# Stick-breaking mixer: projection tiles moved against the heads, weights rounded behind each head's logarithm

## The chip, the cores and the metric

One core of a Trainium2 chip. The metric is the device time of one execution in microseconds (us), as the median of the runs of a kernel. Engines are written PE (TensorE), ACT (ScalarE), DVE (VectorE), POOL (GpSimd) and SP (SyncE).

## What is computed

Two transformer blocks run one after the other on 512 tokens of width 1024, in fp32. The change touches the mixer of the second block, a stick-breaking attention with 16 heads of 64:

```
qkv = xn @ w_qkv;  q, k = rms_norm over each head's 64;  z = q.k / 8, for s < t
log_1m = log_sigmoid(-z);  rev_excl = sum of log_1m over the keys between s and t
w = exp(log_sigmoid(z) + rev_excl);  o = w @ v;  x = x + o @ w_o
```

Everything else (two blocks' feed-forward parts with 2816 hidden units, the first mixer, the norms) is the same in both kernels.

## The kernel before

**Products in three parts.** Every fp32 matrix product is made of three float32r matmuls: a value is split into a rounded part hi and the rest lo, and hi*hi, lo*hi and hi*lo are added in PSUM (`unit`, L333 to L335; in the heads `three`, L576 to L578).

**Units.** All weights come as one stream of units of 128x1024 in four slots. SP loads a unit into `raw` (L272). ACT rounds it to `w_hi` (`round_weights`, the copy at L696, called by `ahead(u)` for unit u + 2), once the unit four before it has been used. POOL subtracts to get `w_lo` (L307), which takes the units in order, and increments `lo_done`. PE waits for `lo_done` before the first of the eight tiles of a unit (L325). One tile is three matmuls of 512 columns. SP's next load into a slot waits for the same `lo_done`.

**The second mixer.** `w_qkv` is 24 units, three to a pair of heads: the query (3t), the key (3t+1) and the value (3t+2) of pair t. `w_o` is the next eight. While the heads of pair t are computed, PE puts tiles of pair t+1 between their steps; the order is written out by hand on each engine. For a head h:

- PE: `stick_scores` (L580) into four PSUM banks, then 10 projection tiles, `weigh(h-1)` (L610, the previous head's weights times its values), `cumulate(h)` (L598, the sums over keys as matmuls with constant triangles), then 2 projection tiles. `turn_values` (L571, four transposes) stands in the even heads behind two tiles, `head_mean_square` near the end of a head.
- ACT: Abs (L904), Exp (L906) and Ln (L908) over the scores, 128x1280 each, in place of one another in `sb_e`; then rounding of values, weights and squares; the output of the previous head (`round_out`); and, when `cumulate` is done, Exp (L926).
- DVE: the softplus (L1293, one input in PSUM), its rounding `sp_hi` (L1300) and rest `sp_lo` (L1302), then values, squares, outputs and head norms; behind L926 the same split of the weights (L1316, L1318).

`cumulate(h)` waits for `sp_split`, which is `sp_lo` (L600). In an even head ACT rounds two weight units, behind `round_values`; in an odd head one, behind `head_square`. These units are 3t+5 and 3t+6, and 3t+7 (ACT lines 909 to 920): each is rounded one or two heads ahead of its first tile. The loop starts with the units 0 to 4 rounded and 0 to 2 projected. In the last two heads `out_part` (tiles of the output projection, units 24 on, whose tile k needs the heads 2k and 2k+1) takes the place of the projection.

Of the kernel before, what the change touches and what calls it, by code (L numbers as in the profile page):

```python
# [25 lines left out]
P = 128  # L26
# [4 lines left out]
QT = TOK // P  # L31
HD = 64
HEADS = 8
SB_HEADS = 16
# [4 lines left out]
AHEAD = 2  # L39
UK = 8  # L40
# [12 lines left out]
U_QKV = U_FFN3 + FFN_UNITS  # L53
U_SBO = U_QKV + QKV_UNITS
# [56 lines left out]
ENDS = [next(m for m in range(LAST_STEP + 1) if filled(m) >= UK * (n + 1)) for n in range(BETWEEN)]  # L111

FILL = [(10, 2), (10, 2)]

FAR = -1e30
OUTSIDE = -3.0e38
# [9 lines left out]
def build(nc, ctx, weights, consts, consts_b, ropes, rel, gain_cols, head_gains, x, out):  # L128
# [37 lines left out]
    at = [region]  # L166
# [151 lines left out]
    def _(pe):  # L318
# [278 lines left out]

        def cumulate(h):  # L598

            pe.wait_ge(S["sp_split"], h + 1)  # L600
            for j in range(QT):
                for k in range(j, QT):
                    to = col[j] + P * (k - j)
                    for part in sp:
                        last = pe.matmul(ps_flat[:, to:to + width[k]], (minus_upto_r if k == j else minus_ones_r),  # L605
                                         part[:, col[k]:col[k] + width[k]],
                                         start=False, stop=True, skip_group_check=True)
            last.then_inc(S["cum_done"], 1)
# [19 lines left out]
        def mixer_2():  # L628
            pairs = SB_HEADS // 2
            pe.wait_ge(S["x_updated"], DT * (FFN_RES[2] + 1))  # L630
            project(0, 2 * UK + 3)
            head_mean_square(0, 0)
            project(2 * UK + 3, 2 * UK + 5)
            head_mean_square(0, 1)
            project(2 * UK + 5, 3 * UK)
            for h in range(SB_HEADS):
                t, odd = divmod(h, 2)
                at = (3 * (t + 1)) * UK + 12 * odd
                before, behind = FILL[odd]
                stick_scores(h)  # L640
                if t + 1 < pairs:
                    if odd:
                        project(at, at + before)
                    else:
                        project(at, at + 2)
                        turn_values(t)
                        project(at + 2, at + before)
                else:
                    if not odd:
                        turn_values(t)  # L650
                    if h == SB_HEADS - 2:
                        pe.wait_ge(*evacuated_2(3 * pairs - 1))
                    if h == SB_HEADS - 1:
                        pe.wait_ge(S["sv_split"], pairs)
                    out_part(2 * odd, 0, pairs - 2)
                    out_part(2 * odd + 1, 0, 3)
                if h:
                    weigh(h - 1)
                if odd and t + 1 < pairs:
                    head_mean_square(t + 1, 1)  # L660
                cumulate(h)
                if t + 1 < pairs:
                    project(at + before, at + before + behind)
                    if not odd:
                        head_mean_square(t + 1, 0)
                else:
                    out_part(2 * odd + 1, 3, pairs - 2)
            for n in range(2):
                out_part(n, pairs - 2, pairs - 1)
            weigh(SB_HEADS - 1)  # L670
            for n in range(2, 4):
                out_part(n, pairs - 2, pairs - 1)
            for n in range(4):
                out_part(n, pairs - 1, pairs)
            for n in range(4, DT):
                out_part(n, 0, DT)
# [17 lines left out]
    def _(act):  # L694
# [163 lines left out]
        def mixer_2():  # L858
            pairs = SB_HEADS // 2

            def head_square(t, c):
                act.wait_ge(S["qk_made"], 2 * t + c + 1)
                nc.scalar.activation(scratch[:, 4 + c, :], scratch[:, c, :], ACT.Square)\
                  .then_inc(S["qk_sq_done"], 1)
                if t:
                    act.wait_ge(S["qk_ms"], 2 * t + c - 1)
                act.wait_ge(S["qk_sq_done"], 2 * t + c + 1)
                copy(qk_sq[c][0][:, :], scratch[:, 4 + c, :]).then_inc(S["qk_sq_hi"], 1)

            def head_rms(t, c):  # L870

                act.wait_ge(S["qk_ms"], 2 * t + c + 1)
                nc.scalar.activation(scratch[:, 4 + c, :], PS[:, 6 + c, :], ACT.Ln, bias=eps_col[:, 0:1])\
                  .then_inc(S["qk_ln"], 1)
                act.wait_ge(S["qk_ln"], 2 * t + c + 1)
                nc.scalar.activation(scratch[:, 4 + c, :], scratch[:, 4 + c, :], ACT.Exp, scale=-0.5)\
                  .then_inc(S["qk_inv"], 1)

            def round_values(t):
                act.wait_ge(S["sv_turned"], t + 1)  # L880
                copy(sb_v[0][:, t % 2, :, :], PS[:, 6, :].rearrange("p (i n) -> p i n", i=QT))\
                    .then_inc(S["sv_hi"], 1)

            def round_out(h):
                r = HD * (h % 2)
                act.wait_ge(S["sb_pv"], h + 1)
                copy(so_hi[r:r + HD, h // 2, :], PS[r:r + HD, 3, :]).then_inc(S["so_hi_done"], 1)

            ahead(U_QKV)
            root_mean_square(S_FFN3)  # L890
            ahead(U_QKV + 1)

            act.preload_act_table_set("natural_log_exp_and_others")
            head_square(0, 0)
            head_square(0, 1)
            ahead(U_QKV + 2)
            head_rms(0, 0)
            head_rms(0, 1)
            for h in range(SB_HEADS):
                t, odd = divmod(h, 2)  # L900
                act.wait_ge(S["z_done"], h + 1)
                if h:
                    act.wait_ge(S["w_split"], h)
                nc.scalar.activation(sb_e[:, :], ps_flat[:, 0:SBW], ACT.Abs).then_inc(S["abs_done"], 1)  # L904
                act.wait_ge(S["abs_done"], h + 1)
                nc.scalar.activation(sb_e[:, :], sb_e[:, :], ACT.Exp, scale=-1.0).then_inc(S["e_done"], 1)  # L906
                act.wait_ge(S["e_done"], h + 1)
                nc.scalar.activation(sb_e[:, :], sb_e[:, :], ACT.Ln, bias=one_col[:, 0:1]).then_inc(S["l_done"], 1)  # L908
                if not odd:
                    round_values(t)  # L910
                    if t + 1 < pairs:
                        ahead(U_QKV + 3 * (t + 1))
                        ahead(U_QKV + 3 * (t + 1) + 1)
                        head_square(t + 1, 0)
                    else:
                        ahead(U_SBO)
                        ahead(U_SBO + 1)
                elif t + 1 < pairs:
                    head_square(t + 1, 1)
                    ahead(U_QKV + 3 * (t + 1) + 2)  # L920
                if h:
                    round_out(h - 1)
                if odd and t + 1 < pairs:
                    head_rms(t + 1, 1)
                act.wait_ge(S["cum_done"], h + 1)
                nc.scalar.activation(sb_e[:, :], ps_flat[:, 0:SBW], ACT.Exp).then_inc(S["w_done"], 1)  # L926
                if not odd and t + 1 < pairs:
                    head_rms(t + 1, 0)
            round_out(SB_HEADS - 1)
            for k in range(DT):  # L930
                if k + 2 < DT:
                    ahead(U_SBO + k + 2)
                tail(k, k % 2, MIX_RES[1], T_MIX2, S_MIX2)
# [29 lines left out]
    def _(dve):  # L963
# [270 lines left out]
        def mixer_2():  # L1234
# [52 lines left out]
            zero_ssq(S_MIX2)  # L1287
            for h in range(SB_HEADS):
                t, odd = divmod(h, 2)
                if odd and t + 1 < pairs:  # L1290
                    make(t + 1, 1)
                dve.wait_ge(S["l_done"], h + 1)
                nc.vector.scalar_tensor_tensor(sb_e[:, :], ps_flat[:, 0:SBW], 0.0, sb_e[:, :], ALU.max, ALU.add)\  # L1293
                    .then_inc(S["sp_done"], 1)
                if odd and t + 1 < pairs:
                    split_squares(t + 1, 1)
                dve.wait_ge(S["sp_done"], h + 1)
                if h:
                    dve.wait_ge(S["cum_done"], h)
# [3 lines left out]
                    .then_inc(S["sp_split"], 1)  # L1303
                if not odd:
                    split_values(t)
                if not odd and t + 1 < pairs:
                    make(t + 1, 0)
                    split_squares(t + 1, 0)
                if h:
                    split_out(h - 1)  # L1310
                if odd and t + 1 < pairs:
                    head_norm(t + 1, 1)
                dve.wait_ge(S["w_done"], h + 1)
                if h:
# [2 lines left out]
                dve.wait_ge(S["w_hi_done"], h + 1)  # L1317
                nc.vector.tensor_tensor(sb_w[1][:, :], sb_e[:, :], sb_w[0][:, :].bitcast(F32), ALU.subtract)\  # L1318
                    .then_inc(S["w_split"], 1)
                if t + 1 < pairs:  # L1320
                    if odd:
                        make(t + 1, 2)
                    else:
                        head_norm(t + 1, 0)
            split_out(SB_HEADS - 1)
            for k in range(DT):
                update(k, (k + 4) % 8, U_SBO + k + 1, 1.0, MIX_RES[1], T_MIX2, S_MIX2, k % 2)
# [32 lines left out]
def mean_bank(stat):  # L1360


    return 7 if stat == S_FFN3 else 4


def index_steps(n):
# [90 lines left out]
```

## Time and profile before

| | us |
|---|---|
| median of 3 runs (2284.69 to 2287.91) | 2285.65 |
| the profiled execution's own time | 2284.73 |
| its span in the trace | 2282.9 |
| PE busy | 2215.4 |
| ACT, DVE, POOL busy | 778.8, 813.9, 867.7 |

The profiled execution lies 0.9 us below the median, and its span 1.8 us below its own time. The mixer's first scores start 1573 us into the span; its output projection ends at 1913. In the trace, idle time stands in square brackets with what ended it. The granted clock (PEclk) is 1.00 where TensorE has its full 2.4 GHz and 0.50 at 1.2 GHz. The ends of matmuls are modelled: one of 512 columns is shown as 0.39 us while the next starts 0.23 us after it.

### The profile page before, as it was taken

The page shows a single profiled execution, that of the slowest core. Times are in us where ns is not written, and L with a number is a line of the kernel's source. Part 1 is how long each engine was busy: PE and PEld are TensorE (multiplying, and loading weights), DVE is VectorE, ACT ScalarE, POOL GpSimd, SP SyncE. Part 2 cuts the span into 40 slices and gives each one's busy share as a digit, 9 for nine tenths or more (in the row PEclk, how much of TensorE's full clock was granted, in tenths as well). Part 3 has the DMA queues.
Part 4 walks back from the last instruction along what each step waited for, and adds up shares of the span by engine and source line. Part 5 has one row for each costly group of instructions (what it writes and reads, how often), then busy time and mean ns, then how long its engine had stood idle before and what let it go on. Part 6 is the DMA issues. An engine that isn't in the chain of part 4 may idle for free. (4 is left out here: it accounts for less than half of the span.)

```text
span 2282.9 us, 27488 instructions
## 1 busy us (share of the span) xinstructions
PE 2215.4 (97%) x9986; PEld 1800.9 (79%) x9986; DVE 813.9 (36%) x1159; ACT 778.8 (34%) x1065; POOL 867.7 (38%) x363
## 2 busy tenths in 40 slices
PE   7999999999999999999999999998989898999999
PEld 6888887676777888888878888887777777888887
DVE  5222112586322432222125222114677655222200
ACT  4223222234333442222333232224545544232221
POOL 4444444331222444444544444443121214444443
PEclk9999999999999999999999999999999999999999
DMA  4332324211111222323332322332111102322332
GB/s 156 101 101 92 110 98 138 81 65 38 51 52 56 92 92 94 103 98 101 103 100 93 101 92 92 106 106 74 37 47 37 47 28 83 101 92 92 101 116 78
DMA packets 56045, 196.53 MB, mean 86 GB/s; under 512 B 6384, under 2 KB 6768, under 8 KB 55984
## 3 DMA queue, kind: packets, MB, share of 16 engines
q1 hardware_dynamic: 54720, 192.93, 25.6%
q10 hardware_dynamic: 1264, 2.75, 0.4%
q8 instruction: 43, 0.70, 0.1%
q14 instruction: 18, 0.15, 0.0%
HBM read 193.43 MB, written 2.10 MB: 86 GB/s over the span
## 5 line engine op out<-in xcount | busy, mean ns | idle before, releaser
L307 POOL TENSOR_TENSOR w_lo<-raw,w_hi 128x1024 fp32r<-128x1024 f32 x359 | 867.5, 2428 | 1396.4 <-ACT w_hi L696 1395.0
L333 PE MATMUL ps<-xn_hi,w_hi 128*128 128x512 f32 x1912 | 765.4, 400 | 17.4 <-DVE xn_lo L997 9.2
L334 PE MATMUL ps<-xn_lo,w_hi 128*128 128x512 f32 x1912 | 748.2, 391 | 0.0
L335 PE MATMUL ps<-xn_hi,w_lo 128*128 128x512 f32 x1912 | 748.2, 391 | 0.0
L333 PEld LDWEIGHTS ps<-xn_hi,w_hi 128*128 128x128 f32 x1912 | 361.2, 189 | 126.0 <-issue 41.9
L335 PEld LDWEIGHTS ps<-xn_hi,w_lo 128*128 128x128 f32 x1912 | 360.9, 189 | 76.8
L334 PEld LDWEIGHTS ps<-xn_lo,w_hi 128*128 128x128 f32 x1912 | 361.7, 189 | 73.4 <-issue 2.6
L696 ACT ACTIVATE w_hi<-raw 128x1024 fp32r<-128x1024 f32 x359 | 364.7, 1048 | 129.9 <-PE ps L335 118.3
L965 DVE TENSOR_TENSOR scratch<-ps,rstd 128x512 f32<-128x512 f32 x207 | 142.6, 690 | 594.1 <-PE ps L335 593.6
L333 PE MATMUL ps<-h_hi,w_hi 128*128 128x512 f32 x704 | 274.0, 389 | 0.0
L334 PE MATMUL ps<-h_lo,w_hi 128*128 128x512 f32 x704 | 274.0, 389 | 0.0
L335 PE MATMUL ps<-h_hi,w_lo 128*128 128x512 f32 x704 | 274.0, 389 | 0.0
L696 ACT ACTIVATE h_hi<-scratch 128x512 f32 (+1 forms) x88 | 55.6, 632 | 476.1 <-DVE scratch L965 476.1
L1058 DVE SCALAR_TENSOR_TENSOR x_sb<-ps,x_sb 128x512 f32 (+1 forms) x48 | 33.1, 690 | 412.0 <-PE ps L335 412.0
L335 PEld LDWEIGHTS ps<-h_hi,w_lo 128*128 128x128 f32 x704 | 132.2, 188 | 27.4
L333 PEld LDWEIGHTS ps<-h_hi,w_hi 128*128 128x128 f32 x704 | 132.2, 188 | 27.3
L334 PEld LDWEIGHTS ps<-h_lo,w_hi 128*128 128x128 f32 x704 | 132.2, 188 | 27.3
L758 ACT ACTIVATE scratch<-scratch 128x512 f32<-128x512 f32 x88 | 55.6, 632 | 180.1 <-DVE scratch L965 180.1
L732 ACT ACTIVATE scratch<-x_sb 128x512 f32 (+1 forms) x40 | 25.3, 632 | 267.4 <-DVE x_sb L1058 267.4
L1012 DVE TENSOR_TENSOR h_lo<-scratch,h_hi 128x512 f32 (+1 forms) x88 | 61.0, 693 | 80.4 <-ACT h_hi L696 80.4
L605 PE MATMUL ps<-sp_hi,const_r 128*128 128x128 f32 (+3 forms) x160 | 54.8, 361 | 33.3 <-DVE sp_lo L1302 33.3
L605 PEld LDWEIGHTS ps<-sp_hi,const_r 128*128 128x128 f32 x160 | 38.0, 237 | 38.8 <-DVE sp_lo L1302 37.8
(179 smaller groups left out, 1832.1 us busy)
## 6 DMA issues: line engine op xcount, KB each, us to landing
raw<-weights SPq DMA_DIRECT2D x359, 512.0 KB, 3.4
x_sb<-x_t SPq DMA_DIRECT2D x8, 256.0 KB, 6.0
bias<-rel ACTq DMA_DIRECT2D x1, 2048.0 KB, 10.1
out_t<-x_sb SPq DMA_DIRECT2D x8, 256.0 KB, 4.7
rope<-ropes ACTq DMA_DIRECT2D x1, 512.0 KB, 3.6
const<-consts SPq DMA_DIRECT2D x1, 192.0 KB, 7.3
to_round<-consts SPq DMA_DIRECT2D x1, 192.0 KB, 7.5
ki<-ki ACTq DMA_DIRECT2D x1, 128.0 KB, 2.2
```

The source lines that it names most:

```text
L307: nc.gpsimd.tensor_tensor(w_lo[s][:, :, :], raw[s][:, :, :], w_hi[s][:, :, :].bitcast(F32), ALU.subtract).then_inc(S["lo_done"], 1)
L333: pe.matmul(to, w_hi[s][:, k, :], hi, start=opens, stop=False)
L334: pe.matmul(to, w_hi[s][:, k, :], lo, start=False, stop=False)
L335: last = pe.matmul(to, w_lo[s][:, k, :], hi, start=False, stop=ends)
L605: last = pe.matmul(ps_flat[:, to:to + width[k]], (minus_upto_r if k == j else minus_ones_r), part[:, col[k]:col[k] + width[k]], start=Fals ...
L696: return nc.scalar.activation(dst, src, ACT.Copy)
L732: nc.scalar.activation(scratch[:, 4 + b, :], X[:, k, :], ACT.Square).then_inc(S["sq_done"], 1)
L758: nc.scalar.activation(scratch[:, j, :], scratch[:, j, :], ACT.Silu).then_inc(S["silu_done"], 1)
L965: return nc.vector.tensor_tensor(dst, p, q, ALU.mult)
L1012: nc.vector.tensor_tensor(h_lo[:, F, :], scratch[:, 2 + j, :], h_hi[:, F, :].bitcast(F32), ALU.subtract).then_inc(S["h_lo_done"], 1)
L1058: nc.vector.scalar_tensor_tensor(X[:, k, :], PS[:, bank, :], factor, X[:, k, :], ALU.mult, ALU.add).then_inc(S["x_updated"], 1)
```

## The change

Head h has the same number of tiles as before, 12 to a head, but six tiles more are done ahead of the loop, so every tile stands six places earlier against the heads: an even head now has the last two tiles of unit 3t+3, all of 3t+4 and two of 3t+5, and an odd head the other six of 3t+5 and six of 3t+6. `head_mean_square` stands behind `cumulate` in the even heads. `cumulate` takes all products with `sp_hi` first, and waits for `sp_lo` only for the second half. ACT rounds unit 5 ahead of the loop; in the loop the weights that `rounded_behind(h - 1)` names are rounded right behind head h's Ln: unit 3t+6 in an odd head, 3t+4 and 3t+5 in an even one (none in head 0), and 24 in head 13, 25 to 27 in head 14. DVE moves projections, squares and norms in the same way, and `split_out(h-1)` behind the split of head h's weights. In the last heads the parts of the output projection stand in another order.

The diff's core, in the order PE, ACT (from `head_rms(0, 0)` on), DVE (from the removed `make(t + 1, 1)` on), new function:

```diff
-FILL = [(10, 2), (10, 2)]
...
 def cumulate(h):
-            pe.wait_ge(S["sp_split"], h + 1)
-            for j in range(QT):
-                for k in range(j, QT):
-                    to = col[j] + P * (k - j)
-                    for part in sp:
+            for part, ready in ((sp[0], S["sp_hi_done"]), (sp[1], S["sp_split"])):
+                pe.wait_ge(ready, h + 1)
+                for j in range(QT):
+                    for k in range(j, QT):
+                        to = col[j] + P * (k - j)
...
-            project(2 * UK + 5, 3 * UK)
+            project(2 * UK + 5, 3 * UK + 6)
             for h in range(SB_HEADS):
                 t, odd = divmod(h, 2)
-                at = (3 * (t + 1)) * UK + 12 * odd
-                before, behind = FILL[odd]
+                at = 3 * (t + 1) * UK
+                more = t + 1 < pairs
                 stick_scores(h)
-                if t + 1 < pairs:
-                    if odd:
-                        project(at, at + before)
+                if not odd:
+                    if more:
+                        project(at + 6, at + 8)
+                    turn_values(t)
+                    if more:
+                        project(at + 8, at + 16)
                     else:
-                        project(at, at + 2)
-                        turn_values(t)
-                        project(at + 2, at + before)
+                        pe.wait_ge(*evacuated_2(3 * pairs - 1))
+                        out_part(1, 0, pairs - 2)
+                        out_part(3, 0, 4)
+                elif t + 2 < pairs:
+                    project(at + 18, at + 28)
+                elif more:
+                    project(at + 18, at + 24)
+                    out_part(0, 0, 4)
                 else:
-                    if not odd:
-                        turn_values(t)
-                    if h == SB_HEADS - 2:
-                        pe.wait_ge(*evacuated_2(3 * pairs - 1))
-                    if h == SB_HEADS - 1:
-                        pe.wait_ge(S["sv_split"], pairs)
-                    out_part(2 * odd, 0, pairs - 2)
-                    out_part(2 * odd + 1, 0, 3)
+                    pe.wait_ge(S["sv_split"], pairs)
+                    out_part(2, 0, pairs - 2)
+                    out_part(0, pairs - 2, pairs - 1)
                 if h:
                     weigh(h - 1)
-                if odd and t + 1 < pairs:
+                cumulate(h)
+                if not odd and more:
+                    head_mean_square(t + 1, 0)
+                    project(at + 16, at + 18)
                     head_mean_square(t + 1, 1)
-                cumulate(h)
-                if t + 1 < pairs:
-                    project(at + before, at + before + behind)
-                    if not odd:
-                        head_mean_square(t + 1, 0)
-                else:
-                    out_part(2 * odd + 1, 3, pairs - 2)
-            for n in range(2):
+                elif not odd:
+                    out_part(3, 4, pairs - 2)
+                elif t + 2 < pairs:
+                    project(at + 28, at + 30)
+                elif more:
+                    out_part(0, 4, pairs - 2)
+            for n in range(1, 4):
                 out_part(n, pairs - 2, pairs - 1)
             weigh(SB_HEADS - 1)
-            for n in range(2, 4):
-                out_part(n, pairs - 2, pairs - 1)
...
             head_rms(0, 0)
             head_rms(0, 1)
+            ahead(U_QKV + 3)
...
                 nc.scalar.activation(sb_e[:, :], sb_e[:, :], ACT.Ln, bias=one_col[:, 0:1]).then_inc(S["l_done"], 1)
+                for n in rounded_behind(h - 1):
+                    ahead(U_QKV + n - AHEAD)
                 if not odd:
+                    if more:
+                        head_square(t + 1, 0)
                     round_values(t)
-                    if t + 1 < pairs:
-                        ahead(U_QKV + 3 * (t + 1))
-                        ahead(U_QKV + 3 * (t + 1) + 1)
-                        head_square(t + 1, 0)
-                    else:
-                        ahead(U_SBO)
-                        ahead(U_SBO + 1)
-                elif t + 1 < pairs:
-                    head_square(t + 1, 1)
-                    ahead(U_QKV + 3 * (t + 1) + 2)
+                elif more:
+                    head_rms(t + 1, 1)
                 if h:
                     round_out(h - 1)
-                if odd and t + 1 < pairs:
-                    head_rms(t + 1, 1)
+                if not odd and more:
+                    head_square(t + 1, 1)
...
-                if odd and t + 1 < pairs:
-                    make(t + 1, 1)
+                if not odd and more:
+                    make(t + 1, 0)
...
-                if odd and t + 1 < pairs:
-                    split_squares(t + 1, 1)
...
                 if not odd:
                     split_values(t)
-                if not odd and t + 1 < pairs:
-                    make(t + 1, 0)
-                    split_squares(t + 1, 0)
-                if h:
-                    split_out(h - 1)
-                if odd and t + 1 < pairs:
+                    if more:
+                        split_squares(t + 1, 0)
+                        make(t + 1, 1)
+                        split_squares(t + 1, 1)
+                elif more:
+                    head_norm(t + 1, 0)
                     head_norm(t + 1, 1)
...
-                if t + 1 < pairs:
-                    if odd:
-                        make(t + 1, 2)
-                    else:
-                        head_norm(t + 1, 0)
+                if odd and more:
+                    make(t + 1, 2)
+                if h:
+                    split_out(h - 1)
...
+def rounded_behind(h):
+
+    t, odd = divmod(h, 2)
+    first = 3 * (t + 2)
+    if h < 0 or h >= SB_HEADS - 3:
+        return range(first + 1, first + 4) if h == SB_HEADS - 3 else range(0)
+    return range(first + 1, first + 3) if odd else range(first, first + 1)
```

## Rows read from the trace of the kernel before

**Rows 1.** The page, part 1: busy us, share of the span, instructions.
```profile
PE 2215.4 (97%) x9986; PEld 1800.9 (79%) x9986; DVE 813.9 (36%) x1159; ACT 778.8 (34%) x1065; POOL 867.7 (38%) x363
```

**Rows 2.** Waits of PE, 1560 to 1900 us: total us, times, longest.
```profile
PE ps L605 <- DVE sp_lo L1302: 33.3, 15, 3.1
PE ps L576 <- DVE sb_k_lo L1263: 2.8, 1, 2.8
PE ps L333 <- POOL w_lo L307: 1.6, 1, 1.6
...
PE ps L576 <- DVE sb_w_lo L1318: 0.2, 1, 0.2
```

**Rows 3.** Timeline of an even head, ACT, DVE, POOL: start, us, engine, line.
```profile
1691.36 1.24 ACT L904 ACTIVATE sb_e<-ps 128x1280 f32<-128x1280 f32 x1 [2.60 <-PE ps L595]
...
1693.94 1.37 ACT L908 ACTIVATE sb_e<-sb_e,one_col 128x1280 f32<-128x1280 f32 x1
...
1695.34 1.49 DVE L1293 SCALAR_TENSOR_TENSOR sb_e<-ps,sb_e 128x1280 f32<-128x1280 f32 x1 [3.59 <-ACT sb_e L908]
1695.68 2.00 ACT L696 ACTIVATE w_hi<-raw 128x1024 fp32r<-128x1024 f32 x2
...
1696.81 5.29 POOL L307 TENSOR_TENSOR w_lo<-raw,w_hi 128x1024 fp32r<-128x1024 f32 x2 [13.71 <-ACT w_hi L696]
...
1696.87 3.03 DVE L1300 CAST sp_hi<-sb_e 128x1280 fp32r<-128x1280 f32 x1
1699.93 3.52 DVE L1302 TENSOR_TENSOR sp_lo<-sb_e,sp_hi 128x1280 fp32r<-128x1280 f32 x1
```

**Rows 4.** Timeline of PE in the same head.
```profile
1691.05 0.27 PE L595 MATMUL ps<-const_b 128*128 128x256 bf16 x1
...
1692.54 0.60 PE L571 MATMUL ps<-const,scratch 128*128 128x128 f32 x4
1692.89 0.47 PE L333 MATMUL ps<-xn_hi,w_hi 128*128 128x512 f32 x1
...
1694.36 0.39 PE L333 MATMUL ps<-xn_hi,w_hi 128*128 128x512 f32 x1
...
1695.04 0.39 PE L333 MATMUL ps<-xn_hi,w_hi 128*128 128x512 f32 x1
...
1703.51 0.79 PE L605 MATMUL ps<-sp_hi,const_r 128*128 128x512 f32 x1 [3.04 <-DVE sp_lo L1302]
```

**Rows 5.** The next, odd head, and all of POOL's instructions by duration.
```profile
1717.33 1.04 ACT L696 ACTIVATE w_hi<-raw 128x1024 fp32r<-128x1024 f32 x1
...
1718.22 0.82 DVE L1300 CAST sp_hi<-sb_e 128x1280 fp32r<-128x1280 f32 x1
...
1718.45 2.84 POOL L307 TENSOR_TENSOR w_lo<-raw,w_hi 128x1024 fp32r<-128x1024 f32 x1 [16.35 <-ACT w_hi L696]
...
L307 POOL TENSOR_TENSOR w_lo<-raw,w_hi x359: 2340/2400/2942, 5.5 to 2261.9; 128x1024 fp32r<-128x1024 f32 x180
```

**Rows 6.** Stretches: us; PE, PEld, DVE, ACT, POOL busy; granted clock; DMA.
```profile
1573.00:1864.00 291.00, 257.19 (x1287) 218.56 (x1288) 199.52 (x174) 145.17 (x161) 62.17 (x23) 0.93 0.13 42
...
1703.40:1706.60 3.20, 3.10 (x10) 2.91 (x11) 1.78 (x4) 1.80 (x3) 0.00 (x0) 0.50 0.40 154
...
1723.40:1726.80 3.40, 3.40 (x25) 3.12 (x23) 1.62 (x3) 1.08 (x1) 0.00 (x0) 1.00 0.20 82
1573.70:1580.30 6.60, 6.60 (x24) 5.68 (x24) 0.34 (x1) 3.46 (x3) 0.00 (x0) 0.50 0.01 2
1583.00:1592.00 9.00, 5.88 (x34) 4.98 (x33) 7.54 (x5) 1.40 (x4) 4.52 (x2) 1.00 0.34 117
```

**Rows 7.** Timeline of the last head's end, ACT and DVE.
```profile
1878.95 1.24 ACT L926 ACTIVATE sb_e<-ps 128x1280 f32<-128x1280 f32 x1 [2.34 <-PE ps L605]
...
1881.09 1.49 DVE L1318 TENSOR_TENSOR sb_w_lo<-sb_e,sb_w_hi 128x1280 fp32r<-128x1280 f32 x1
1884.80 0.59 ACT L696 ACTIVATE so_hi<-ps 64x512 fp32r<-64x512 f32 x1 [4.61 <-PE ps L578]
1885.43 0.69 DVE L1274 TENSOR_TENSOR so_lo<-ps,so_hi 64x512 fp32r<-64x512 f32 x1 [2.85 <-ACT so_hi L696]
```

More of the change, by code:

```diff
@@ L898, in mixer_2 @@
             head_rms(0, 1)
+            ahead(U_QKV + 3)
             for h in range(SB_HEADS):
                 t, odd = divmod(h, 2)
+                more = t + 1 < pairs
                 act.wait_ge(S["z_done"], h + 1)
@@ L1289, in mixer_2 @@
                 t, odd = divmod(h, 2)
-                if odd and t + 1 < pairs:
-                    make(t + 1, 1)
+                more = t + 1 < pairs
+                if not odd and more:
+                    make(t + 1, 0)
                 dve.wait_ge(S["l_done"], h + 1)
@@ L1305, in mixer_2 @@
                     split_values(t)
-                if not odd and t + 1 < pairs:
-                    make(t + 1, 0)
-                    split_squares(t + 1, 0)
-                if h:
-                    split_out(h - 1)
-                if odd and t + 1 < pairs:
+                    if more:
[4 more added lines that the diff above has]
+                    head_norm(t + 1, 0)
                     head_norm(t + 1, 1)
```

## The prediction

> **What bounds the kernel now.** I read the page first: PE is busy for 2215.4 of 2282.9 us [rows 1], so what an edit is worth is read from PE's idle time and from its clock. The waits of PE over the mixer come next: 33.3 us in 15 waits before `cumulate`, all for `sp_lo`, then 2.8 before the first scores, and 1.6 and 0.2 near the end [rows 2]. The timeline of an even head shows why the longest are 3.0 us: POOL's two subtractions and DVE's `sp_hi` and `sp_lo` run at the same time, and DVE's take 3.03 and 3.52 us [rows 3] where `sp_hi` takes 0.82 in an odd head, in which it starts before POOL [rows 5]. L1293, which reads PSUM, takes 1.49 beside nothing and is not held up [rows 3]. PE arrives 3.04 us early [rows 4]. The stretches show a second price: behind the 2.8 us wait the clock is 0.50 for 6.6 us, behind the 3.04 us wait for 3.2 us; it stays 1.00 about the first head's 3.1 us wait and behind a short one of 1.3 us [rows 6]. The mean of 0.93 over 291 us [rows 6] means 0.07 x 2 x 291 = 41 us at 1.2 GHz, which is eight falls of 5.1 us; about 38 of them are busy time, so 19 us are lost to it.
>
> **What the change takes away.** With six tiles more ahead of the loop (6 x 0.68 = 4.1 us, the pitch of a tile being 1695.04 - 1694.36 [rows 4]), the first scores wait less. But unit 5's subtraction now runs about 1570.6 to 1573.0, in the middle of the second head norm, and holds up its last three DVE steps (0.75, 0.43 and 0.69 us by the neighbouring steps' sizes, an estimate): 0.8 of the 2.8 us stay. The waits for `sp_lo` all go (33.3 us), as the next part shows: PE comes to `cumulate` later than `sp_lo` ends. The split of `cumulate` in two halves, costed at nothing, is hidden by that same lateness.
>
> **What it adds: the weights come late.** `rounded_behind(h - 1)` names the units that head h itself uses. In an odd head unit 3t+6 is rounded behind that head's Ln and its first tile is the seventh of the ten in front; in an even head from the third on unit 3t+4 is rounded there and its first tile stands behind only two tiles and four transposes. I count from the end of the scores, Z = 1691.05 + 0.27 = 1691.32 [rows 4]. Ln ends at 1693.94 + 1.37 = 1695.31 [rows 3], Z + 4.0. The rounding takes 1.04 and POOL starts 0.08 behind it (1717.33 + 1.04 against 1718.45) [rows 5]; a subtraction by itself takes 2.40, the median of 359 [rows 5]. DVE's `sp_hi` comes only behind L1293's 1.49 us, 0.4 us behind POOL's start, so POOL goes first. Ready: Z + 4.0 + 1.04 + 0.08 + 2.40 = Z + 7.5.
>
> - Even heads 2 to 12, six of them: PE is at this unit at 1692.89 [rows 4], Z + 1.6. It waits 5.9, shown as some 5.6 since the modelled end lies later.
> - Odd heads 1 to 13, seven: six tiles, Z - 0.2 + 4.1 = Z + 3.9; it waits 3.6, shown as 3.3.
> - Head 14: `out_part(1)` needs unit 25 behind the transposes alone: 6.4; and unit 27, the third of three subtractions, another 0.8 (less than its lateness, as PE's six tiles between are at the low clock).
> - Sum: 6 x 5.6 + 7 x 3.3 + 6.4 + 0.8 = 63.9 us.
>
> What stands behind these waits: on PE the rest of the head, `weigh`, `cumulate` and the next scores, and behind them ACT's Exp (L926) and Abs; nothing can make it up, since both chains start from the same scores. `sp_lo` is hidden: in an even head 8 tiles and `weigh` took from 1692.89 to 1700.47 (1703.51 - 3.04) [rows 4], 7.6 us, so PE reaches `cumulate` at Z + 15.1, and `sp_lo` ended at Z + 12.1 (1699.93 + 3.52) [rows 3]. In an odd head 4 tiles and `weigh` put it at Z + 12.3, `sp_lo` at about Z + 9.8. The late unit of an even head also makes its key squares late, but these are needed only behind `cumulate`.
>
> **The end.** Behind the last `cumulate`, Exp, `sb_w_hi`, `sb_w_lo` end at 1881.09 + 1.49 = 1882.58, 3.6 us behind 1878.95 [rows 7]. Now `split_out(14)` with 0.69 comes behind that, and PE has three tiles, 2.05, instead of five: 2.2 us of wait instead of 0.2. Behind the last `weigh` no tile is left to cover `so_hi` and `so_lo`, 0.59 + 0.69 with their hand-offs from 1884.76 to 1886.12 [rows 7]: 1.3 us. Together +3.3. The 1.6 us for POOL stays.
>
> **Moved at no cost.** Unit 5's rounding one step earlier: ACT has its two norm steps done by then. Its load and the next one of SP's queue, and POOL's turn, come earlier by it; POOL is busy 62 of 291 us here [rows 6]. The loads of later units are triggered by later subtractions, but each slot is still filled a head or more ahead. `head_square`, `head_rms`, `make` and the squares on ACT and DVE lie under PE's longer head. DVE is busy for 199.5 of 291 us [rows 6]; if the cover went, `sp_lo` would be late next.
>
> **The clock.** The trace has no waits of 3.3 and 5.6 us in front of projections. The bounds: nothing more than now (the same eight falls), or every one of 14 such waits followed by a long stretch, 14 x 6.6 / 2 = 46, 27 more than now. Eight of nine waits of 2.8 to 3.1 us were followed by a fall, so I take 14 falls; and for each the shorter length, 3.4 us, as in a longer wait a part of the slow stretch lies in the wait: 14 x 3.4 / 2 = 24, which is 4.6 more than the 19.2 of now (38.4 / 2).
>
> **Sum.** Idle: 63.9 + 0.8 - 2.8 - 33.3 + 3.3 = +31.9. Clock +4.6. Together +36.5 on the profiled execution's own 2284.7; the median lies 0.9 above it: 2285.65 + 36.5 = 2322.1 us, slower by 1.6%.
>
> **Rivals.**
>
> - **The units are there in time** (faster). If a unit's subtraction ended before PE comes to it, that is within 1.6 us of the scores in an even head and 3.9 in an odd one, only the gain would be left. It takes PE's 33.3 to about 0.9 in each even head (`cumulate`'s second half at Z + 10.8 against `sp_lo` at Z + 11.7), 7 in all, and leaves no wait that lowers the clock: -26.3 - 2.0 + 3.3 - 19.2 = -44, 2241 us. For it: POOL is idle for four fifths and was waited for once [rows 2, 6]. Against: Ln alone ends at Z + 4.0 [rows 3], and ACT goes in order, so no unit of this head can be rounded before. If the new function does something else than I read (units of the next head), this would be the case. 3%.
> - **The odd heads' waits don't lower the clock** because they lie unluckily, as the first head's 3.1 us did: seven falls fewer, 7 x 3.4 / 2 = 12 less: 2310 us. 9%.
> - **The slow stretches are the long ones**: +27 instead of +4.6: 2345 us. For it: the 6.6 us behind the first scores [rows 6]. 8%.
> - **POOL is slowed beside DVE.** A subtraction next to `sp_hi` took 2.84 instead of 2.40 [rows 5]. If all 14 late units met this: 14 x 0.44 = +6.2, 2328 us. Against: in the odd row DVE had started 0.23 us before POOL, and now POOL would be 0.4 us ahead. The Trainium skill bears on this one in a sentence of its own: "GPSIMD Engine Reference", "Specifications", says that GpSimd shares its SBUF interfaces with VectorE and contends with instructions in a two-port mode or with two SBUF inputs; read as a rule for every overlap it gives this rival's 2328 rather than 2322. By that rule, which the trace bears out with 1.49 us for L1293 in every head, the first subtraction is free of DVE for the 0.4 us. 12%.
>
> **How the numbers follow.** My own case has 67%. The likeliest case gives 2322. The range takes in the third and fourth case by half of the clock's bound, 2322 + 14 = 2336, and goes down past the second to 2309; the 3% of a gain and most of the longest clock case lie outside. About 0.2%, 4.6 us, is what a measurement of this kernel can tell from no change: slower by more than that 0.96, within it 0.01, faster 0.03.
>
> **What would show it.** Right: waits of PE's L333 on POOL's `w_lo` L307 of about 64 us in some 15 pieces, 3.3 in the odd and 5.6 in the even heads; none of L605 on `sp_lo` or a few tenths; POOL's `w_lo` starting 5.1 us behind the scores in every head; 14 stretches at 0.50. It ends with a wait of L576 on DVE of about 2.2. Wrong: waits on POOL below 10 us, which would mean that the units were rounded a head earlier; or waits as forecast with a clock of 1.00 behind them, or of 0.50 through half of the mixer.

## The result and the profile after

The changed kernel takes 2321.57 us (median of 4 runs, 2320.59 to 2324.08) against 2285.66 before: the ratio is 1.0157, with a 95% interval of 1.014 to 1.0175. It is slower by 35.9 us; the forecast was 36.5.

Page, part 1, after, behind its first line. It answers to [rows 1]: PE is busy 5.8 us longer, and the span is 39.4 us longer, so 33.6 us of it are idle time. The profiled execution was the slowest of the four.

```profile
span 2322.3 us, 27488 instructions
...
PE 2221.2 (96%) x9986; PEld 1801.0 (78%) x9986; DVE 807.6 (35%) x1159; ACT 777.8 (33%) x1065; POOL 864.8 (37%) x363
```

Waits of PE in the mixer, 1560 to 1960 us, after (total, times, longest), against [rows 2]. L331, L574 and L603 are the former L333, L576 and L605; L305 is POOL's subtraction, the former L307.

```profile
PE ps L331 <- POOL w_lo L305: 59.8, 15, 5.7
PE ps L331 <- issue: 6.3, 1, 6.3
...
PE ps L574 <- DVE so_lo L1273: 2.3, 1, 2.3
PE ps L331 <- DVE so_lo L1273: 1.4, 1, 1.4
PE ps L574 <- DVE sb_k_lo L1262: 0.8, 1, 0.8
```

The 33.3 us of waits for `sp_lo` are gone from the list: no wait of L603 is left. In their place stand 59.8 us for `w_lo`; 1.6 of them are the old wait near the end, and the 6.3 us that the view puts down to "issue" are head 14's wait for unit 25, whose `w_lo` ends in that moment. Late weights cost 59.8 - 1.6 + 6.3 = 64.5 us.

The timeline of an even head after, the one that [rows 3, 4] show of before; the first fence is ACT, DVE and POOL, the second PE.

```profile
1707.57 1.36 ACT L911 ACTIVATE sb_e<-sb_e,one_col 128x1280 f32<-128x1280 f32 x1
1708.84 1.99 ACT L697 ACTIVATE w_hi<-raw 128x1024 fp32r<-128x1024 f32 x2
1708.96 1.49 DVE L1293 SCALAR_TENSOR_TENSOR sb_e<-ps,sb_e 128x1280 f32<-128x1280 f32 x1 [1.90 <-ACT sb_e L911]
1709.96 5.26 POOL L305 TENSOR_TENSOR w_lo<-raw,w_hi 128x1024 fp32r<-128x1024 f32 x2 [17.97 <-ACT w_hi L697]
1710.49 2.50 DVE L1298 CAST sp_hi<-sb_e 128x1280 fp32r<-128x1280 f32 x1
...
1713.03 3.54 DVE L1300 TENSOR_TENSOR sp_lo<-sb_e,sp_hi 128x1280 fp32r<-128x1280 f32 x1
```

```profile
1704.69 0.27 PE L593 MATMUL ps<-const_b 128*128 128x256 bf16 x1
...
1706.18 0.60 PE L569 MATMUL ps<-const,scratch 128*128 128x128 f32 x4
1712.46 0.76 PE L331 MATMUL ps<-xn_hi,w_hi 128*128 128x512 f32 x1 [5.68 <-POOL w_lo L305]
...
1721.36 1.54 PE L603 MATMUL ps<-sp_hi,const_r 128*128 128x512 f32 x10
```

The scores end at 1704.96. Ln ends 4.0 us later, POOL starts 1.0 behind it, and the first tile of the late unit runs at 1712.46, 7.5 us behind the scores. `cumulate` starts at 1721.36 with no idle time ahead of it; `sp_lo` had ended at 1716.57, 4.8 us earlier. The odd heads show the same with 3.4 us of wait.

Stretches after (us; PE, PEld, DVE, ACT, POOL busy; granted clock; DMA), against [rows 6]: the whole of the heads, and the first scores with what follows.

```profile
1573.00:1904.00 331.00, 265.22 (x1302) 220.79 (x1301) 193.06 (x176) 142.32 (x159) 58.89 (x23) 0.89 0.12 38
1576.00:1584.00 8.00, 7.16 (x33) 5.97 (x33) 3.12 (x6) 4.39 (x4) 0.00 (x0) 0.79 0.22 66
```

A mean of 0.89 means 0.11 x 2 x 331 = 73 us at 1.2 GHz, where it was 41. Much of it lies in the waits, in which it costs nothing.

### The profile page after: what moved, and what is told of

Same layout as the page of the kernel before. It is cut to its first block and busy times, and to the rows that moved or that the text cites. A ratio compares the mean times of both kernels' runs of the same rounds, so it can differ in the third digit from the quotient of the medians.

```text
span 2322.3 us, 27488 instructions
## 1 busy us (share of the span) xinstructions
PE 2221.2 (96%) x9986; PEld 1801.0 (78%) x9986; DVE 807.6 (35%) x1159; ACT 777.8 (33%) x1065; POOL 864.8 (37%) x363
## 3 DMA queue, kind: packets, MB, share of 16 engines
q1 hardware_dynamic: 54720, 192.93, 25.1%
## 5 line engine op out<-in xcount | busy, mean ns | idle before, releaser
L305 POOL TENSOR_TENSOR w_lo<-raw,w_hi 128x1024 fp32r<-128x1024 f32 x359 | 864.6, 2420 | 1438.6 <-ACT w_hi L697 1437.1
L331 PE MATMUL ps<-xn_hi,w_hi 128*128 128x512 f32 x1912 | 773.5, 405 | 72.3 <-POOL w_lo L305 54.3
L333 PE MATMUL ps<-xn_hi,w_lo 128*128 128x512 f32 x1912 | 753.7, 394 | 0.0
L331 PEld LDWEIGHTS ps<-xn_hi,w_hi 128*128 128x128 f32 x1912 | 365.4, 191 | 186.2 <-issue 91.3
L333 PEld LDWEIGHTS ps<-xn_hi,w_lo 128*128 128x128 f32 x1912 | 364.3, 191 | 78.9
L331 PE MATMUL ps<-h_hi,w_hi 128*128 128x512 f32 x704 | 274.0, 389 | 0.0
L333 PE MATMUL ps<-h_hi,w_lo 128*128 128x512 f32 x704 | 274.0, 389 | 0.0
L331 PEld LDWEIGHTS ps<-h_hi,w_hi 128*128 128x128 f32 x704 | 132.2, 188 | 27.4
L333 PEld LDWEIGHTS ps<-h_hi,w_lo 128*128 128x128 f32 x704 | 132.2, 188 | 27.2
L964 DVE TENSOR_TENSOR scratch<-scratch 128x512 f32<-128x512 f32 x89 | 61.8, 695 | 9.2
L697 ACT ACTIVATE scratch<-ps 128x128 f32<-128x128 f32 (+3 forms) x64 | 27.8, 434 | 89.5 <-PE ps L507 89.4
```

Of the source, the lines that this page charges most:

```text
L305: nc.gpsimd.tensor_tensor(w_lo[s][:, :, :], raw[s][:, :, :], w_hi[s][:, :, :].bitcast(F32), ALU.subtract).then_inc(S["lo_done"], 1)
L331: pe.matmul(to, w_hi[s][:, k, :], hi, start=opens, stop=False)
L333: last = pe.matmul(to, w_lo[s][:, k, :], hi, start=False, stop=ends)
L697: return nc.scalar.activation(dst, src, ACT.Copy)
L964: return nc.vector.tensor_tensor(dst, p, q, ALU.mult)
```

## The experiments

For each run I split the span of its profiled execution into PE's busy time and the rest (page, part 1). As all kernels run the same 9986 matmuls, I read a difference in busy time as what the clock costs; it resolves some 2 us, since e2 and e9 differ by 1.7 with an edit that cannot touch it.

| kernel | time, us | span | PE busy | rest |
|---|---|---|---|---|
| before | 2285.66 | 2282.9 | 2215.4 | 67.5 |
| changed | 2321.57 | 2322.3 | 2221.2 | 101.1 |
| e1, next head's units behind Ln | 2260.17 | 2258.6 | 2206.6 | 52.0 |
| e2, the same units behind the second Exp | 2239.67 | 2237.9 | 2199.1 | 38.8 |
| e3, before with halves | 2261.89 | 2261.0 | 2210.6 | 50.4 |
| e4, odd heads' units early | 2293.34 | 2292.7 | 2215.5 | 77.2 |
| e5, before, rounding first | 2276.75 | 2276.3 | 2213.3 | 63.0 |
| e6, spread rounding | 2251.05 | 2249.4 | 2198.9 | 50.5 |
| e7, e2 without halves | 2241.87 | 2239.3 | 2198.5 | 40.8 |
| e8, e6 with unit 5 in the loop | 2251.30 | 2250.6 | 2201.3 | 49.3 |
| e9, e2 with the end mended | 2237.85 | 2236.1 | 2197.4 | 38.7 |
| e10, even heads' units early | 2273.73 | 2272.6 | 2209.3 | 63.3 |

**e1: the same place, the next head's units.** The changed kernel with one argument changed.

```diff
-                for n in rounded_behind(h - 1):
+                for n in rounded_behind(h):
                     ahead(U_QKV + n - AHEAD)
```

> The changed kernel, but behind head h's logarithm the units of head h+1 are rounded, not those of head h (the new function is called with h). Theory (the late units are the whole loss): no wait of PE on POOL inside the heads; an odd head now has two subtractions beside its softplus split, so the second half of its cumulate waits about 1.8 us (7 x 1.8 = 12 us); no low clock in the heads but the one behind the first scores; about 2247 us. Rival (the loss lies in the new order of the tiles or in POOL running beside DVE right behind the logarithm): waits move to sp_lo in the same size as before, 33 us, and the low stretches stay; about 2285 us or more.

2260.17 us, ratio to before 0.9887 (0.9869 to 0.9904). The waits for weights in the heads are gone, and with them 61 us against the changed kernel. So what costs is above all which unit is rounded there; the place itself is worth the 20.5 us by which e2 is faster. The time is 13 us above the expectation. Part of it stands in the waits of PE (1560 to 1960 us):

```profile
PE ps L603 <- DVE sp_lo L1300: 11.6, 7, 1.7
PE ps L574 <- DVE sb_k_lo L1262: 5.7, 5, 2.8
```

The seven waits for `sp_lo` came as expected; the second line did not. Two subtractions in an odd head push the head norms back, and the next scores wait for them; the 2.8 us are behind head 13, which has three. Most of the rest is the clock: PE is busy 7.5 us longer than in e2. It did not stay up behind every 1.7 us wait, against what I wrote, while it did behind the first scores, where I had a fall. The granted clock in the 3.3 us behind the second and the third of these waits:

```profile
1641.30:1644.60 3.30, 3.30 (x13) 3.06 (x14) 3.16 (x6) 0.93 (x1) 0.00 (x0) 0.58 0.38 139
1676.70:1680.00 3.30, 3.03 (x16) 2.38 (x16) 3.16 (x6) 1.25 (x1) 0.00 (x0) 1.00 0.38 139
```

**e2: the same units at the end of the head before.**

```diff
                 nc.scalar.activation(sb_e[:, :], sb_e[:, :], ACT.Ln, bias=one_col[:, 0:1]).then_inc(S["l_done"], 1)
-                for n in rounded_behind(h - 1):
-                    ahead(U_QKV + n - AHEAD)
...
                 if not odd and more:
                     head_rms(t + 1, 0)
+                for n in rounded_behind(h):
+                    ahead(U_QKV + n - AHEAD)
```

> The changed kernel, but the same units are rounded at the end of the head before, behind its second Exp, away from the softplus split. Theory: units in time and POOL nowhere beside sp_hi and sp_lo, so no wait in the heads at all, no low clock behind them: 2285.7 - 33.3 - 2.0 + 3.3 (the end) - 17.5 (clock) = about 2236 us. Rival (the rounding at this place delays ACT's Abs of the next head, or POOL holds up the split of the weights): a wait of some 1 to 2 us in each head turns up on another line, 2250 to 2265 us.

2239.67 us, ratio 0.980 (0.9783 to 0.9818). PE's waits in the heads are six of 0.4 us for `w_lo`, and 1.0 and 0.3 in head 14; the clock from 1573 to 1820 us is 0.99. The expected 2236 left these small waits out: a subtraction that starts 0.12 us behind the second step of the weights' split takes 3.62 us instead of 2.40, while the split keeps its 1.49 (last two rows, from the timelines). Against the changed kernel this moves nothing but the roundings, and is 82 us faster.

```profile
PE ps L331 <- POOL w_lo L305: 4.4, 8, 1.6
PE ps L574 <- DVE so_lo L1273: 2.3, 1, 2.3
PE ps L331 <- DVE so_lo L1273: 1.4, 1, 1.4
PE ps L331 <- issue: 1.0, 1, 1.0
```

```profile
1639.33 1.49 DVE L1316 TENSOR_TENSOR sb_w_lo<-sb_e,sb_w_hi 128x1280 fp32r<-128x1280 f32 x1
1639.45 3.62 POOL L305 TENSOR_TENSOR w_lo<-raw,w_hi 128x1024 fp32r<-128x1024 f32 x1 [12.54 <-ACT w_hi L697]
```

**e4 and e10: one kind of late unit at a time.** The changed kernel; in e4 the odd heads' unit is rounded in the even head before, in e10 (`if odd:` in place of `if not odd:`) the even heads' units in the odd head before.

```diff
-                for n in rounded_behind(h - 1):
-                    ahead(U_QKV + n - AHEAD)
+                if not odd:
+                    for n in (*rounded_behind(h - 1), *rounded_behind(h)):
+                        ahead(U_QKV + n - AHEAD)
```

> The changed kernel, but the unit that an odd head needs is rounded in the even head before it, behind the even head's own units; only the even heads' units come late. Theory: the seven waits of 3.4 us go with their seven low stretches (1.65 us each), the even heads' waits of 5.7 us stay: 2321.6 - 23.6 - 11.5 = about 2286 us. Rival (a 5.7 us wait brings a longer low stretch when no other is near it): 2290 to 2300 us.

> The mirror of the run in which the odd heads' units were early: here only the odd heads' unit comes late, and the even heads' units are rounded behind it in the same odd head. Theory: seven waits of 3.4 us stay, the 5.7 us ones go; three subtractions in an odd head push sp_lo and the head norms back, so that some 1.5 us of wait for sb_k_lo come before six of the next scores; with low clock behind each 3.4 us wait at 1.7 us lost or more: 2239.7 + 24 + 12 to 16 + 9 = 2285 to 2289 us. Rival (a 3.4 us wait lowers the clock only where a 5.7 us wait stands near it): about 2273 us.

e4: 2293.34 us, ratio 1.0036 (1.0024 to 1.0047). e10: 2273.73, ratio 0.9948 (0.9933 to 0.9963). Waits of PE for `w_lo`, first e4, then e10:

```profile
PE ps L331 <- POOL w_lo L305: 35.0, 7, 5.7
PE ps L331 <- issue: 6.3, 1, 6.3
```

```profile
PE ps L331 <- POOL w_lo L305: 25.1, 8, 3.4
PE ps L574 <- DVE sb_k_lo L1263: 4.9, 3, 3.1
```

The waits are the expected ones, six of 5.7 us and head 14's in e4, seven of 3.4 in e10 (25.1 less the old 1.6 is 23.5). In e4 the rest falls by 23.9 us against the changed kernel, 23.6 expected. The clock is what both missed. Busy time above that of e2 is 16.4 us in e4 and 10.2 in e10; I had put 11.5 us of gain on the odd heads in e4 and it was 5.7. In e10 I had also doubled the waits for `sb_k_lo`, 9 for a measured 4.1 above the first scores' 0.8, and had added the late waits to e2's time without taking off the small ones that they replace, some 3 us.

e4's time is that of its rival, and the rows bear it out in five of the seven late heads. Behind the ends of the late waits PE is busy at 0.50 for 3.8, 5.1, 5.8, 6.1, 2.9, 4.7 and 5.6 us, 34 in all, so 17 us are lost, 2.4 a head; the changed kernel has 3.1 to 3.3 behind the same waits. Their length is the same, so the length alone does not set the price: the slow stretch starts 3.0, 1.7, 1.0, 0.7, 0.5, 2.2 and 4.6 us ahead of the wait's end, and only what is left of it behind the end is paid. Here are the first late wait, from 1611.95 to 1617.63, from the inside and behind it, and the time behind the fourth, which ended at 1738.15. Whether the odd heads' waits decide where a stretch starts was not tried.

```profile
1615.00:1617.00 2.00, 0.00 (x0) 0.00 (x0) 1.97 (x2) 2.00 (x4) 1.87 (x1) 0.50 0.00 0
1617.70:1621.00 3.30, 3.30 (x8) 2.62 (x9) 3.27 (x2) 0.97 (x2) 3.27 (x2) 0.50 0.48 159
1738.15:1744.29 6.14, 6.14 (x15) 4.79 (x16) 6.11 (x4) 1.04 (x2) 6.14 (x2) 0.50 0.51 171
```

The rival of e10, that short waits lower the clock only beside long ones, names the measured time but falls: behind each of e10's first three 3.4 us waits the clock is 0.58 to 0.69 on the mean of some 3.3 us. In all a fall follows five of the seven; the fourth and the seventh have none. These are the first and the fourth.

```profile
1600.60:1604.00 3.40, 3.40 (x10) 2.64 (x11) 3.37 (x2) 0.48 (x1) 3.40 (x2) 0.58 0.48 159
1712.30:1715.60 3.30, 3.30 (x15) 2.67 (x15) 3.27 (x2) 0.33 (x1) 3.26 (x2) 1.00 0.51 159
```

**e3 and e5: two parts of the change alone, in the kernel before.** e3 takes over the two halves of `cumulate`, as the change has them. e5 rounds the units of before directly behind Ln:

```diff
                 if not odd:
+                    ahead(U_QKV + 3 * (t + 1))
+                    ahead(U_QKV + 3 * (t + 1) + 1)
                     round_values(t)
                     if t + 1 < pairs:
-                        ahead(U_QKV + 3 * (t + 1))
-                        ahead(U_QKV + 3 * (t + 1) + 1)
                         head_square(t + 1, 0)
...
                 elif t + 1 < pairs:
+                    ahead(U_QKV + 3 * (t + 1) + 2)
                     head_square(t + 1, 1)
-                    ahead(U_QKV + 3 * (t + 1) + 2)
```

> The kernel before with one part of the change alone: cumulate takes the products with sp_hi first and waits for sp_lo behind them. Theory: the hi half (10 matmuls, 1.4 us) fills the 1.3 us waits of the odd heads and leaves 1.6 us of the 3.0 in the even ones: -20 us of idle time; waits of 1.6 us don't lower the clock, another -16: about 2250 us. Rival (the clock falls behind 1.6 us waits as well): about 2266 us. Rival (sp_hi itself ends too late to help in the even heads): about 2275 us.

> The kernel before with another part of the change alone: the same units as before are rounded directly behind each head's logarithm, ahead of the values and the squares. Theory: POOL starts 0.5 us earlier in the even heads and about 1 us in the odd ones, and now goes ahead of sp_hi in both; sp_lo ends 0.3 us earlier in the even heads (POOL's two subtractions still stand around it) and 0.7 in the odd ones: 7 to 8 us of waits fewer, the low stretches as before, about 2278 us. Rival (the place directly behind the logarithm itself holds up the softplus split, by POOL): later by up to 1.6 us in each odd head, 2290 to 2297 us.

e3: 2261.89 us, ratio 0.9897 (0.988 to 0.9915). The time lies between the expected 2250 and the rival's 2266. The waits for `sp_lo` fall to 13.8 us in 8 pieces (expected 13), all in even heads. But the clock falls behind some of the 1.7 us waits and not behind others, so each of the two cases holds in part: the first row is behind the wait that ended at 1695.18, the second behind the one at 1730.82.

```profile
1695.20:1698.50 3.30, 3.30 (x12) 3.11 (x13) 1.85 (x4) 2.00 (x4) 0.00 (x0) 0.52 0.41 150
1730.90:1734.00 3.10, 2.96 (x16) 2.31 (x16) 1.68 (x3) 1.86 (x4) 0.00 (x0) 1.00 0.38 145
```

e5: 2276.75 us, ratio 0.9961 (0.9945 to 0.9976). The time is the expected 2278 within 2 us, but the waits for `sp_lo` are 28.6 us instead of 33.3, 4.7 less where I had put 7 to 8. Rounding right behind Ln is a small gain by itself (0.4%) as long as the units are those of a later head. Both parts are sound; neither is what made the changed kernel slow.

**e6 and e8: two attempts to better e2 that failed.** e6 rounds an odd head's first unit ahead of the second Exp and puts `split_out(14)` back in front of the last split; e8 moves unit 5 into head 0 as well.

```diff
+                if odd:
+                    for n in rounded_behind(h)[:1]:
+                        ahead(U_QKV + n - AHEAD)
                 act.wait_ge(S["cum_done"], h + 1)
```

> The kernel that rounds behind the second Exp, with two changes: in odd heads the first of the units is rounded already behind the rounding of the previous head's output, ahead of the second Exp; and split_out(14) stands ahead of the split of the last head's weights. Theory: the seven waits of 0.4 us and the 1.3 us of head 14 go, and 0.7 us at the end: 2239.7 - 4.9 = about 2235 us. Rival (POOL's subtraction now holds up the head norms or the split of the weights on DVE, so that the next scores are late): 2240 us or more.

> As the run with spread rounding and the mended end, but unit 5 is rounded in head 0 behind the values and not ahead of the loop, so that its subtraction no longer stands in the second head norm. Theory: the 0.84 us wait before the first scores goes, and the low stretch behind these scores (3.4 us, 1.7 lost) with it: 2.5 us less than that run, about 2232.5 us. Rival (the clock falls behind these scores without any wait, since their matmuls use 64 of 128 rows): only 0.8 us less.

2251.05 and 2251.30 us (ratios 0.9844, 0.9831 to 0.9857, and 0.985, 0.9837 to 0.9864). e6's rival came true. Its timeline at the end of an odd head, POOL and DVE:

```profile
1637.85 2.40 POOL L305 TENSOR_TENSOR w_lo<-raw,w_hi 128x1024 fp32r<-128x1024 f32 x1 [9.15 <-ACT w_hi L697]
1637.94 2.60 DVE L1263 CAST sb_k_hi<-scratch 128x512 fp32r<-128x512 f32 x1
...
1641.26 2.97 POOL L305 TENSOR_TENSOR w_lo<-raw,w_hi 128x1024 fp32r<-128x1024 f32 x1 [1.01 <-ACT w_hi L697]
1642.04 3.55 DVE L1321 TENSOR_TENSOR sb_w_lo<-sb_e,sb_w_hi 128x1280 fp32r<-128x1280 f32 x1
```

`sb_k_hi`, 0.43 us by itself, takes 2.60, and `sb_w_lo`, 1.49 by itself, takes 3.55: each started 0.1 to 0.8 us behind a subtraction and ended with or after it. The next scores wait 0.9 us for `sb_k_lo` and the transposes 1.1 for the values. In e8 the first scores wait for nothing, but unit 5's subtraction now holds up the squares; what it gains (rest -1.2) the clock takes back. The stretch at 0.50 that both of its cases were about was not there to be had: behind e6's first scores the clock is 1.00, for all its wait of 0.85 us.

**e7 and e9: parts of e2.** e7 takes the halves out of e2, e9 puts `split_out(14)` ahead of the last head's split.

```diff
+                if h == SB_HEADS - 1:
+                    split_out(h - 1)
                 dve.wait_ge(S["w_done"], h + 1)
...
-                if h:
+                if 0 < h < SB_HEADS - 1:
                     split_out(h - 1)
```

> The kernel that rounds behind the second Exp, with cumulate as before: hi and lo in turn, one wait for sp_lo. Theory: sp_lo ends 7.9 us behind the scores and PE comes to cumulate at 8.7 or later, so the halves bring nothing there: 2239 to 2241 us. Rival (the halves still cover something in the first or last heads): 2241 to 2245 us.

> The kernel that rounds behind the second Exp, with one change: split_out(14) stands ahead of the split of the last head's weights, as it did before the change. Theory (the 2.3 us wait before the last weigh is 3.6 us of Exp and split plus 0.7 of split_out, less three tiles): that wait is 1.6 us, 0.7 us less in all, about 2239.0 us. Rival (the last weights' split waits for split_out in turn, since both are DVE's): no change, 2239.7.

e7: 2241.87 us, ratio 0.981 (0.9796 to 0.9823). The intervals of e2 and e7 overlap, so the waits decide: those for `sp_lo` are 0.7 us in head 0 and 1.3 in head 15 and were nothing in e2, so the halves are worth 2 us there, the rival's case; I had overlooked that head 0 has no `weigh` and head 15 fewer tiles. e9: 2237.85 us, ratio 0.9797 (0.9784 to 0.9811). The wait before the last `weigh` is 1.6 us instead of 2.3, as expected; the rest of its 1.8 us against e2 is not resolved (their profiles differ by 1.7 us of busy time, which the edit cannot touch). It is the fastest version here, 48.0 us below the kernel before as run beside it (2285.88) and 83.7 below the changed one.

## Why the prediction was right

**The late units, 63.9 us: 64.5 measured.** The count from the scores (4.0 + 1.04 + 0.08 + 2.40 = Z + 7.5) met the timeline to 0.1 us. Single waits: 5.7 in the even heads (5.6 forecast), 3.4 in the odd (3.3), 6.3 in head 14 (6.4), 0.6 for unit 27 (0.8). e1 and e2 show the cause: with the next head's units in place of this head's, these waits go.

**The waits for `sp_lo`, -33.3: gone**, and hidden by the margin that I worked out: `cumulate` came 4.8 us behind `sp_lo`, where 3.0 was forecast (PE 1.3 us later, as the tiles behind its wait ran at the low clock, and `sp_lo` 0.5 us earlier).

**The first scores, 0.8 of 2.8 us left: 0.8. The end, +3.3: +3.5** (2.3 + 1.4 against 0.2). The e9 run shows the `split_out` part by itself.

**The clock, +4.6: about +5.** The rest of the span's 39.4 us divides so: the mixer starts 1.8 us later than in the profiled execution of before, PE's waits in the mixer add 71.1 - 38.4 = 32.7 (with 0.5 for the transposes in both), which leaves 4.9. The stretches at 0.50, taken one by one, say the same: PE is busy in them for 51.7 us in the mixer and for 42.2 before, and half of the difference is 4.8.

The step was right too: a fall behind each of the 14 late waits, and in the longer waits a part of the slow stretch lies in the wait. The rows are an odd head's stretch, and an even head's, up to the end of its 5.7 us wait and behind it.

```profile
1691.72:1695.13 3.41, 3.00 (x7) 2.45 (x8) 3.34 (x4) 0.00 (x0) 0.27 (x1) 0.50 0.40 150
1708.79:1712.46 3.67, 0.00 (x1) 0.03 (x1) 3.46 (x2) 3.58 (x6) 2.50 (x2) 0.50 0.01 2
1712.46:1715.61 3.15, 3.15 (x8) 2.47 (x9) 3.12 (x2) 0.09 (x1) 2.76 (x1) 0.50 0.52 166
```

Behind all 14, PE is busy for 3.0 to 3.3 us at 0.50, 43.6 in all, where I had 14 x 3.4 = 47.6. There was also a fifteenth stretch, 3.4 us behind the first scores, which I had not counted; the two misses cancel. And it was luck that one price served for both kinds of wait. The slow stretch started 3.6 to 3.7 us ahead of the end of each of the seven long waits here; in e4, with the same waits, it was 0.5 to 4.6 us, and a long wait cost 2.4 us of busy time instead of 1.6. My working could not tell the two apart.

**The sum.** On the profiled executions the terms give 64.5 - 33.3 - 2.0 + 3.5 + 4.9 = 37.6 us, and 39.4 with the 1.8 from ahead of the mixer; the medians differ by 35.9. The forecast of 36.5 lies between. That it met the medians to 0.6 us is luck, as the four runs of the changed kernel lie within 3.5 us of each other.

**The rivals.** The units in time would give 2241 us, I wrote; e2 does that and measures 2239.67. The odd heads' waits do lower the clock. The slow stretches lasted 6.8 us in the even heads, but half of each lay in the wait, so the longest price was not paid. POOL was not slowed by starting ahead of DVE: the odd heads' subtractions took 2.34 us, and DVE's `sp_hi` beside them 2.49, so DVE bore the overlap and the 2328 us of that rival fell with its 2.84. The 1.49 us of L1293 that I gave against it as borne out by the trace of before showed nothing yet: there L1293 ends 0.02 us behind POOL's start [rows 3]. After, the two overlap by 0.5 us (1709.96 to 1710.45), and it still takes 1.49.

## What to carry to other kernels

When work is moved against a stream of prepared weights, count for each unit from the event that both chains share: here the scores, with preparation ready 7.5 us behind and the first use at 1.6 or 3.9. The engine's idle share tells nothing about this: POOL was free for four fifths of the time and was waited for 64.5 us. An order that hides the old wait can be right and still lose: the same order with its roundings one head earlier is 2% faster than before, not 1.6% slower. And look at which of two contending engines starts first: behind Ln (e1) and ahead of the second Exp (e6) POOL's subtraction started first and held up a split that PE waits for; behind the second Exp (e2) the split started 0.12 us ahead, the subtraction took the delay, and PE waited for it for 0.4 us in six heads.

## What was not expected of the hardware

- **The clock fell behind a wait of 0.84 us.** In the changed kernel the stretch with the first scores has a mean of 0.79: the scores' matmuls behind that wait read 64 rows instead of 128, and the tiles behind them ran with 0.63 us instead of 0.39. Seven other kernels have a wait of 0.8 to 0.9 us at the same place, and only in e2 did a stretch at 0.50 follow it. The rows are the first of the scores' matmuls in the changed kernel, e2's stretch with its scores (0.80), and the 7.7 us behind the wait in e7. Whether the 64 rows play a part was not tried.

```profile
1576.89 0.50 PE L574 MATMUL ps<-sb_q_hi,sb_k_hi 64*128 64x512 f32 x1 [0.84 <-DVE sb_k_lo L1262]
1573.40:1582.00 8.60, 7.76 (x35) 6.47 (x35) 3.64 (x6) 4.88 (x5) 0.00 (x0) 0.80 0.20 61
1575.30:1583.00 7.70, 7.70 (x42) 6.54 (x43) 2.96 (x4) 5.15 (x6) 0.00 (x0) 1.00 0.13 54
```

- **Waits of 1.7 us lowered it in some heads and not in others** (e1, e3: 0.58 and 1.00; 0.52 and 1.00), with the same work ahead of and behind them. This is why a wait's price can't be read from its length alone: in e3 I expected 16 us back from the clock, and PE's busy time fell by 4.8 (2215.4 to 2210.6).
- **An overlap of POOL and DVE costs the one that comes second.** L1293, with one input in PSUM, took 1.49 us in every head, also where POOL started 0.5 us before its end; in the even heads the two steps behind it took 2.50 and 3.54 instead of the 0.83 and 1.49 of head 0, where POOL is idle. The Trainium skill, "GPSIMD Engine Reference", "Specifications", names the shared interfaces, and as what contends the instructions in a two-port mode or with two SBUF inputs. The trace agrees for `sp_lo`, which reads two SBUF tiles and is held up, and for L1293, which reads one and is not; `sp_hi` reads one too and is held up, which by that section would take the two-port mode, and no row here names its mode. The one that started first (the odd heads' subtraction, 2.34 us, no longer than alone) was not slowed.
